# Turning normed rows among the last product steps of each projection in a one-core decoder step

## The chip, the core and the metric

The kernel runs on one core of a Trainium2 chip, in one launch. Its time is device microseconds of that core, the median of several executions. A core has TensorE (PE) for matrix products and transposes, VectorE (DVE), ScalarE (ACT), GpSimd (POOL) and SyncE (SP), which issues most transfers. Each works through its own instructions in order, and they wait for one another by semaphores.

## What is computed

One inference step of a two-layer decoder trunk: 512 prompt rows and 8 x 8 sample rows of width 1024. Layer 0 mixes by block-sparse and sliding-window attention, layer 1 by gated linear attention (GLA). Each layer has a convolutional feed-forward part of inner width 2816. Four times the residual stream goes through a layer norm, after the attention's output projection, after the first down projection, after the GLA output projection and after the second down projection:

```python
xp = layer_norm(DN_ALPHA * xp + mp, ln_mix_g[l], ln_mix_b[l])
fp, cbp = conv_ffn(xp, buf0, ffn_w_up[l], ffn_conv_w[l], ffn_conv_b[l], ffn_w_down[l])
xp = layer_norm(DN_ALPHA * xp + fp, ln_ffn_g[l], ln_ffn_b[l])
```

The output of each of the first three norms is the input of the next projection (up projection of layer 0, GLA's q and k, up projection of layer 1). The fourth is the result.

## The kernel before

**Tiles.** The rows lie in five tiles, 0 to 3 of 128 prompt rows and 4 (PQ) of the 64 sample rows. Products are done in fp32r in three parts: a matrix is split into a high part (rounded, `xh_reg`, `w_hi`) and a low part (what is left, `xl_reg`, `w_lo`), and a step multiplies high by high, high by low and low by high. A weight unit is 512 KB, loaded by SP (L475, L587) into `raw`. ACT makes `w_hi` (L1138, L1283), DVE makes `w_lo` (L1475, L1745), and for the first unit behind a norm POOL makes it (`split_after_norm`, L2052).

**Product steps with a norm behind them** (`products_before_norm`). A step (c, t) multiplies weight unit c with tile t into PSUM bank t, with L669 for prompt tiles and L680 for the sample rows. The last two units are walked as pairs, in the order of `PAIR`; here 0 and 1 stand for the last unit but one and the last:

```python
PAIR = [(0, 0), (0, 1), (1, 0), (0, 2), (1, 1), (0, 3), (1, 2), (0, 4), (1, 3), (1, 4)]
```

For a norm behind two units (stage 0) each is a half of the width, and DVE reads a bank after every step. For stages 1 and 2 both belong to the second half, and DVE reads a bank only after (1, t). A full step of a prompt tile is 12 products of 512 columns, the last of stages 1 and 3 has 6. A step of the sample rows has 8 or 4.

**The norm on DVE** (`residual_ln`). `residual` adds the bank to the residual rows (L1666, for the sample rows also L1670) and takes statistics (L1673). `normalise` joins them (L1679), subtracts the mean and multiplies by the gain (L1684), waits for ACT's square root (L1255, `ln_roots`), and does the rest (L1686, L1688), which signals `ln_done`.

**Turning** (`turn_x`, `turn`, L650). The normed rows have to stand with the width on the partitions. PE transposes a tile in two batches of four 128 x 128 blocks, into PSUM banks 5 and 6 in turn. A batch waits until ACT has copied the one before last out (L1124, `take_x`, the high part), and, where that was a normed tile, until DVE has taken the low part (L1482, `x_los`).

**The hand-over** (`run_here`, `after_ln`, `lo_here`). The first unit behind the norm has four runs, m = 0 to 3, of 24 products of 288 columns. Runs 0 and 1 read columns 0 to 287 (tiles 0, 1 and a part of 2), runs 2 and 3 the rest. Ahead of m = 0 PE waits for this unit's `w_lo`, then turns tiles 0, 1 and 2 and waits for their low parts. Ahead of m = 1 it turns tile 3, ahead of m = 2 tile 4, and it waits there for all parts. DVE has the low parts of tiles 0 to 2 behind the norm of tile 3, and those of 3 and 4 behind the norm of tile 4. ACT copies tiles 0 to 2 behind the root of tile 3, and 3 and 4 behind the root of tile 4. It makes `w_hi` of the next unit behind the root of tile 2, once step (0, 4) has been done.

**Side rows** (`turn_sides`, `take_sides`). The up projections also need 20 rows of convolution state, weights and biases feature-major: two batches of 22 transposes of 20 x 128 blocks. In stages 0 and 2 PE does them just ahead of the step that is fifth from the end, (0, 3), and ACT copies them behind the root of tile 1.

Batches of transposes are numbered in the order in which PE does them (`BATCH_LN0`, `BATCH_LN1`, `BATCH_Y`, `BATCH_LN2`, `LO_BATCHES`), and waits are counted by these numbers.

Of the kernel before, what the change touches and what calls it, by code (L numbers as in the profile page):

```python
# [21 lines left out]
NTILE = len(TILES)  # L22
# [38 lines left out]
KEY_STEPS = [(tile_, g_) for tile_ in range(2) for g_ in range(4)]  # L61
# [24 lines left out]
for k_, n_ in (("attn_out", 2), ("down0", 2 * len(DOWN_GROUPS)), ("gla_out", 4), ("down1", 2 * len(DOWN_GROUPS))):  # L86
    NORM_UNITS.append([UNIT_NO[(k_, c_)] for c_ in range(n_)])
PAIRED = {units_[-2] for units_ in NORM_UNITS}


def freed(n):
# [71 lines left out]
def build_program(nc, io):  # L163
    with ExitStack() as ctx:
# [242 lines left out]
        def query_tile(n):  # L407
# [10 lines left out]
        KEYS_TURNED = {step: BATCH_BEFORE_SAMPLE + sum(2 * GROUP_BLOCKS[g] for _, g in KEY_STEPS[:i + 1])  # L418
                       for i, step in enumerate(KEY_STEPS)}

        BATCH_LN0 = KEYS_TURNED[KEY_STEPS[-1]] + 2 * SP_BATCH + 2
        BATCH_LN1 = BATCH_LN0 + TURNS_X
        BATCH_GLA = BATCH_LN1 + TURNS_X
        BATCH_Y = BATCH_GLA + 2 * GH
        BATCH_LN2 = BATCH_Y + TURNS_X + 2

        LO_BATCHES = ([b for b in range(TURNS_X)]
                      + [b0 + b for b0 in (BATCH_LN0, BATCH_LN1, BATCH_Y, BATCH_LN2) for b in range(TURNS_X)])

        def state_place(n):  # L430

# [206 lines left out]
        def _(pe):  # L638
# [245 lines left out]
            def products_before_norm(stage, groups, before_tile=None):  # L884


                sums = norm_sums(stage)
                for c, t in norm_steps(stage):
                    n = NORM_UNITS[stage][c]
                    half, g = divmod(c, len(groups(0)))  # L890
                    k0, kn = groups(c)[g]
                    unit_here(n)
                    if stage % 2 == 0 and (c, t) == norm_steps(stage)[-5]:
                        turn_sides(stage // 2)
                    if before_tile is not None:
                        before_tile(c, t)
                    if half == 1 and g == 0:
                        pe.wait_ge(z_read, 2 * stage * NTILE + sums.index((0, t)) + 1)
                    project(n, t, k0, kn, g == 0, g == len(groups(0)) - 1)

            def samples_here(c, t):
                if t == PQ:
# [10 lines left out]
            def run_here(m, stage, first_batch):  # L913


                if m == 0:
                    after_ln(stage, range(3))
                    lo_here(first_batch, 6)
                elif m == 1:
                    after_ln(stage, [3])  # L920
                elif m == 2:
                    after_ln(stage, [4])
                    pe.wait_ge(turned_out, first_batch + TURNS_X)
                    lo_here(first_batch, TURNS_X)

            def ffn(l):
# [191 lines left out]
        def _(act):  # L1118
# [132 lines left out]
            def ln_roots(stage):  # L1251
                for t in range(NTILE):
                    n = TILES[t][1]
                    act.wait_ge(ln_var, stage * NTILE + t + 1)
                    act.activation(ln_sd[0:n, t, 0:1], ln_mv[0:n, t, 1:2], ACT.Sqrt, bias=eps_ln[0:n, 0:1]).then_inc(ln_root, 1)  # L1255
                    if stage % 2 == 0 and t == 1:
                        take_sides()
                    if t == 2 and stage < 3:
                        split_hi(NORM_UNITS[stage][-1] + 1)
                    if t == 3 and stage < 3:  # L1260
                        for before in range(3):
                            take_x(before)
                if stage < 3:
                    take_x(3)
                    take_x(4)

            def take_sides():
                for v in range(2):
# [193 lines left out]
        def _(dve):  # L1462
# [23 lines left out]
            def x_los(first_batch, t):  # L1486

                r0, n = TILES[t]
                for half in range(2):
                    k0 = 4 * half  # L1490
                    in_order, beside_hi = xTl[:, k0:k0 + 4, r0:r0 + n], xTh[:, k0:k0 + 4, NT:SLOT]
                    if t < PQ or first_batch in (BATCH_LN0, BATCH_LN2):
                        places = [in_order]
                    elif first_batch == BATCH_LN1:
                        places = [beside_hi, in_order]
                    else:
                        places = [beside_hi]
                    batch_lo(first_batch + 2 * t + half, k0, r0, n, places)

            split_lo(0)  # L1500
            for t in range(NTILE):
# [188 lines left out]
            def residual_ln(stage, duty, first_batch):  # L1690
# [5 lines left out]
                for i, (c, t) in enumerate(norm_steps(stage)):  # L1696
                    if t == 0 and c < len(units) - 1:
                        duty(c)
                    half, late = divmod(c, per_half)
                    if late < per_half - 1:  # L1700
                        continue
                    sums += 1
                    residual(stage, half, t, STEPS_BEFORE[units[0]] + i + 1, 2 * stage * NTILE + sums)
                    if half == 1:
                        normalise(stage, t)
                        if t == 3 and first_batch is not None:

                            for before in range(3):
                                x_los(first_batch, before)
                if first_batch is not None:  # L1710
                    x_los(first_batch, 3)
                    x_los(first_batch, 4)
                    dve.wait_ge(lo_done, units[-1] + 2)

            def units_of(kind, n):
# [474 lines left out]
```

## Time and profile before

| | us |
|---|---|
| median of three executions | 1608.63 (1607.99 to 1610.58) |
| the profiled execution | 1606.65 |
| its span in the profile | 1604.9 |
| PE busy with products and transposes | 1508.3 (94%) |
| DVE busy | 920.0 (57%) |
| ACT busy | 553.4 (34%) |
| POOL busy | 57.1 (4%) |
| share of PE in the chain that ended last | 85% |
| mean granted clock of TensorE | 0.971 |

A timeline row gives start (us from the start of the span), duration, engine, line, operation, output and inputs, sizes, count, and in brackets how long the engine had been idle and what released it. The granted clock is the share of 2.4 GHz, so 0.50 is 1.2 GHz. Matmul ends are modelled, and the next product starts before the last has ended, so the distance of starts is what a product costs.

### The profile page before, as it was taken

Reading aid. Unit: us, or ns where it says so; the run is one execution under the profiler, and the core shown is the slowest. Engines: PE = TensorE matmul, PEld = TensorE weight load, DVE = VectorE, ACT = ScalarE, POOL = GpSimd, SP = SyncE. Lnnn points to the kernel's source line nnn. Section 1 sums busy time; section 2 is a strip of 40 time slices with the busy share of each in tenths; the row PEclk is TensorE's granted clock in tenths of the full one; section 3 lists DMA queues with packets and bytes.
Section 4 is the critical chain, followed back from the end, with each engine's and each line's share of the span. In section 5 each row is a group of like instructions: output and inputs, shape, how many; then the busy total and the mean of one; then the engine's idle time right before and its main releaser. Section 6 shows DMA issues by size and latency. Waiting matters only on the chain.

```text
span 1604.9 us, 24203 instructions
## 1 busy us (share of the span) xinstructions
PE 1508.3 (94%) x9372; PEld 1331.2 (83%) x9372; DVE 920.0 (57%) x1738; ACT 553.4 (34%) x1030; POOL 57.1 (4%) x90
## 2 busy tenths in 40 slices
PE   6999897889999999999799999899899999999995
PEld 5888675669999999878698888668799999998784
DVE  2654253377666666554721776575676666665545
ACT  3222276324333333332225332521243333333321
POOL 0002200010000000000100000000100000000000
PEclk9999999989999999999899999999799999999998
DMA  5225456622223321422211211442022333214211
GB/s 174 102 99 163 115 203 232 171 73 80 79 82 90 88 80 52 129 79 92 78 55 53 79 53 53 136 150 80 27 80 79 84 90 87 79 52 128 79 66 59
DMA packets 153215, 153.56 MB, mean 96 GB/s; under 512 B 12014, under 2 KB 122734, under 8 KB 152910
## 3 DMA queue, kind: packets, MB, share of 16 engines
q1 hardware_dynamic: 149210, 139.47, 28.1%
q0 software_dynamic: 3936, 13.14, 2.6%
q8 instruction: 47, 0.77, 0.2%
q14 instruction: 22, 0.18, 0.0%
HBM read 140.76 MB, written 21.91 MB: 101 GB/s over the span
## 4 chain that ended last, share of the span: by engine, by line
PE 85%; DVE 7%; ACT 3%; SPq 2%; issue 2%; DMA 1%; POOL 0%; ACTq 0%; DVEq 0%; POOLq 0%
PE ps L669 69%; PE ps L680 4%; PE ps L650 4%; PE ps L1026 1%; DVE x_reg L1684 1%; PE ps L737 1%; PE ps L1059 1%; PE ps L771 1%; SPq L522 1%; PE ps L1090 1%; DVE x_reg L1688 1%; DVE w_lo L1475 1%; ACT w_hi L1138 1%; PE ps L947 1%; DVE x_reg L1666 1%
## 5 line engine op out<-in xcount | busy, mean ns | idle before, releaser
L669 PE MATMUL ps<-xh_reg,w_hi 128*128 128x288 f32 x1552 | 465.4, 300 | 8.2 <-DVE xl_reg L1482 8.2
L669 PE MATMUL ps<-xl_reg,w_hi 128*128 128x288 f32 x1552 | 460.8, 297 | 0.0
L669 PE MATMUL ps<-xh_reg,w_lo 128*128 128x288 f32 x1552 | 460.8, 297 | 0.0
L669 PE MATMUL ps<-w_hi,xh_reg 128*128 128x512 f32 x768 | 308.2, 401 | 6.9 <-DVE xl_reg L1726 3.4
L669 PEld LDWEIGHTS ps<-xh_reg,w_hi 128*128 128x128 f32 x1552 | 295.1, 190 | 10.5 <-DVE xl_reg L1482 5.4
L669 PE MATMUL ps<-w_hi,xl_reg 128*128 128x512 f32 x768 | 302.2, 394 | 0.0
L669 PE MATMUL ps<-w_lo,xh_reg 128*128 128x512 f32 x768 | 302.1, 393 | 0.0
L669 PEld LDWEIGHTS ps<-xl_reg,w_hi 128*128 128x128 f32 x1552 | 295.3, 190 | 0.0
L669 PEld LDWEIGHTS ps<-xh_reg,w_lo 128*128 128x128 f32 x1552 | 294.9, 190 | 0.0
L1475 DVE TENSOR_TENSOR w_lo<-raw,w_hi 128x2048 fp32r<-128x2048 f32 (+1 forms) x52 | 113.7, 2186 | 259.1 <-ACT w_hi L1138 259.1
L669 PEld LDWEIGHTS ps<-w_hi,xh_reg 128*128 128x128 f32 x768 | 146.3, 191 | 39.0 <-issue 7.2
L1138 ACT ACTIVATE w_hi<-raw 128x2048 fp32r<-128x2048 f32 (+1 forms) x55 | 100.8, 1833 | 223.2 <-PE ps L680 215.0
L669 PEld LDWEIGHTS ps<-w_hi,xl_reg 128*128 128x128 f32 x768 | 145.9, 190 | 31.4
L1761 DVE TENSOR_SCALAR arena<-arena 128x512 f32<-128x512 f32 (+1 forms) x176 | 67.7, 427 | 179.3 <-ACT arena L1297 179.3
L1763 DVE SCALAR_TENSOR_TENSOR arena<-arena 128x512 f32<-128x512 f32 x352 | 166.8, 515 | 6.3
L669 PEld LDWEIGHTS ps<-w_lo,xh_reg 128*128 128x128 f32 x768 | 146.3, 191 | 28.9
L1296 ACT ACTIVATE arena<-ps 128x224 f32<-128x224 f32 x88 | 31.5, 358 | 239.4 <-PE ps L669 239.4
L1745 DVE TENSOR_TENSOR w_lo<-raw,w_hi 128x2048 fp32r<-128x2048 f32 x44 | 100.5, 2284 | 3.3 <-ACT w_hi L1283 3.1
L1283 ACT ACTIVATE w_hi<-raw 128x2048 fp32r<-128x2048 f32 x44 | 83.7, 1902 | 0.1
L680 PE MATMUL ps<-w_hi,xh_reg 128*128 128x512 f32 x192 | 75.8, 395 | 1.3 <-DVE x_reg L1670 1.3
L650 PE MATMUL ps<-ident,x_reg 128*128 128x128 f32 (+1 forms) x232 | 40.9, 335 | 38.1 <-DVE xl_reg L1482 12.2
L1294 ACT ACTIVATE arena<-ps 128x288 f32<-128x288 f32 x88 | 36.0, 412 | 112.7 <-PE ps L669 112.7
(188 smaller groups left out, 1530.5 us busy)
## 6 DMA issues: line engine op xcount, KB each, us to landing
raw<-in_ffn_w_up SPq DMA_DIRECT2D x88, 512.0 KB, 5.0
raw<-in_ffn_w_down SPq DMA_DIRECT2D x40, 512.0 KB, 4.6
raw<-in_attn_w_in SPq DMA_DIRECT2D x24, 512.0 KB, 4.8
raw<-in_gla_w_in SPq DMA_DIRECT2D x24, 512.0 KB, 4.6
out_swa_s<-in_state_swa_kv SPq DMA_DIRECT2D x2, 3968.0 KB
x_reg<-in_x_prompt SPq DMA_DIRECT2D x8, 512.0 KB, 7.1
raw<-in_gla_w_out SPq DMA_DIRECT2D x8, 512.0 KB, 4.7
out_swa_p<-arena POOLq DMA_DIRECT2D x18, 128.0 KB, 3.0
```

The costliest lines, as they stand in the source:

```text
L522: sp.dma_start(values_of[s][:, b:b + GROUP_BLOCKS[g], :] if g < 3 else values_of[s][:, b, :], src).then_inc(v_cached[s // 4], 16)
L650: last = pe.transpose(ps[0:cols, bank, col:col + rows], src, ident[0:rows, 0:rows])
L669: mm = pe.matmul(out, lhs(i, a), rhs(i, b), start=first and i == 0 and a + b == 0, stop=last and i == ks - 1 and a == 1)
L680: mm = pe.matmul(ps[:, t, :], xTh[:, k0 + i, NP:SLOT], w[b][:, i, :], start=first and i + b == 0, stop=last and i == kn - 1 and b == 1)
L1138: act.activation(w_hi[:, n % 2, 0:a], raw[:, n % 2, 0:a], ACT.Copy).then_inc(hi_done, 1)
L1283: act.activation(w_hi[:, slot, :], raw[:, slot, :], ACT.Copy).then_inc(hi_done, 1)
L1294: act.activation(ext[:, u, v, 2:2 + SPLIT], ps[:, m, 0:SPLIT], ACT.Copy).then_inc(ext_ready, 1)
L1296: act.activation(ext[:, u, v, 2 + SPLIT:2 + NP], ps[:, m, 0:PRE], ACT.Copy)
L1475: dve.tensor_tensor(w_lo[:, n % 2, 0:a], raw[:, n % 2, 0:a], w_hi[:, n % 2, 0:a].bitcast(F32), ALU.subtract).then_inc(lo_done, 1)
L1745: dve.tensor_tensor(w_lo[:, slot, :], raw[:, slot, :], w_hi[:, slot, :].bitcast(F32), ALU.subtract).then_inc(lo_done, 1)
L1761: ins = dve.tensor_scalar(y, e, w, fj[:, u, v, SIDE - 1:SIDE], ALU.mult, ALU.add)
L1763: ins = dve.scalar_tensor_tensor(y, e, w, y, ALU.mult, ALU.add)
```

## The change

In stages 0 to 2 PE turns tile 0 behind step (1, 1), tile 1 behind (1, 2) and tile 2 behind (1, 3), each after a wait for the norm of that tile. At m = 0 it then only waits for the low parts of tiles 0 to 2. The side rows are turned at m = 2, ahead of tile 4. ACT copies tiles 0 and 1 behind their own roots, tile 2 behind `w_hi`, and tile 3 and the side rows behind the root of tile 3, all ahead of the root of tile 4. DVE takes the low parts of tiles 0 and 1 behind the norms of tiles 1 and 2, those of tile 2 ahead of the norm of tile 3, and those of tile 3 ahead of the norm of tile 4. The numbers of the batches follow. Stage 3, which has no projection behind it, stays.

```diff
+TURN_STEPS = (-6, -4, -2)
...
-        BATCH_LN0 = KEYS_TURNED[KEY_STEPS[-1]] + 2 * SP_BATCH + 2
-        BATCH_LN1 = BATCH_LN0 + TURNS_X
+        BATCH_LN0 = KEYS_TURNED[KEY_STEPS[-1]] + 2 * SP_BATCH
+        BATCH_LN1 = BATCH_LN0 + TURNS_X + 2
...
-        BATCH_LN2 = BATCH_Y + TURNS_X + 2
+        BATCH_LN2 = BATCH_Y + TURNS_X
...
-                      + [b0 + b for b0 in (BATCH_LN0, BATCH_LN1, BATCH_Y, BATCH_LN2) for b in range(TURNS_X)])
+                      + [b0 + b + (2 if b0 in (BATCH_LN0, BATCH_LN2) and b >= 8 else 0)
+                         for b0 in (BATCH_LN0, BATCH_LN1, BATCH_Y, BATCH_LN2) for b in range(TURNS_X)])
...
-                    if stage % 2 == 0 and (c, t) == norm_steps(stage)[-5]:
-                        turn_sides(stage // 2)
                     if before_tile is not None:
                         before_tile(c, t)
                     if half == 1 and g == 0:
                         pe.wait_ge(z_read, 2 * stage * NTILE + sums.index((0, t)) + 1)
                     project(n, t, k0, kn, g == 0, g == len(groups(0)) - 1)
+                    for before, at in enumerate(TURN_STEPS):
+                        if stage < 3 and (c, t) == norm_steps(stage)[at]:
+                            pe.wait_ge(ln_done, stage * NTILE + before + 1)
+                            turn_x(before)
...
                 if m == 0:
-                    after_ln(stage, range(3))
                     lo_here(first_batch, 6)
                 elif m == 1:
                     after_ln(stage, [3])
                 elif m == 2:
+                    if stage % 2 == 0:
+                        turn_sides(stage // 2)
                     after_ln(stage, [4])
-                    pe.wait_ge(turned_out, first_batch + TURNS_X)
+                    pe.wait_ge(turned_out, first_batch + TURNS_X + (0 if stage % 2 else 2))
                     lo_here(first_batch, TURNS_X)
...
-                    if stage % 2 == 0 and t == 1:
-                        take_sides()
-                    if t == 2 and stage < 3:
+                    if stage == 3:
+                        continue
+                    if t < 2:
+                        take_x(t)
+                    elif t == 2:
                         split_hi(NORM_UNITS[stage][-1] + 1)
-                    if t == 3 and stage < 3:
-                        for before in range(3):
-                            take_x(before)
-                if stage < 3:
-                    take_x(3)
-                    take_x(4)
+                        take_x(2)
+                    elif t == 3:
+                        take_x(3)
+                        if stage % 2 == 0:
+                            take_sides()
+                    else:
+                        take_x(4)
...
                     if half == 1:
+                        if t >= 3 and first_batch is not None:
+                            x_los(first_batch, t - 1)
                         normalise(stage, t)
-                        if t == 3 and first_batch is not None:
-
-                            for before in range(3):
-                                x_los(first_batch, before)
+                        if 1 <= t < 3 and first_batch is not None:
+                            x_los(first_batch, t - 1)
                 if first_batch is not None:
-                    x_los(first_batch, 3)
-                    x_los(first_batch, 4)
+                    x_los(first_batch, NTILE - 1)
                     dve.wait_ge(lo_done, units[-1] + 2)
```

## Rows read from the trace of the kernel before

**Rows 1.** Waits of PE: who waited for whom, total us, times, longest.
```profile
PE ps L650 <- DVE xl_reg L1482: 14.1, 7, 5.8
```

**Rows 2.** Timeline of PE at the hand-over of stage 0.
```profile
323.41 2.88 PE L650 MATMUL ps<-ident,arena 20*128 20x20 f32 x44 [0.78 <-issue]
326.22 0.80 PE L669 MATMUL ps<-w_hi,xh_reg 128*128 128x512 f32 x1
...
330.63 0.39 PE L669 MATMUL ps<-w_hi,xh_reg 128*128 128x512 f32 x1
...
339.38 0.47 PE L680 MATMUL ps<-w_hi,xh_reg 128*128 128x512 f32 x1 [1.34 <-DVE x_reg L1670]
...
342.48 1.09 PE L650 MATMUL ps<-ident,x_reg 128*128 128x128 f32 x8 [1.02 <-POOL w_lo L2052]
...
351.13 0.61 PE L669 MATMUL ps<-xh_reg,w_hi 128*128 128x288 f32 x1 [1.41 <-DVE xl_reg L1482]
...
357.01 1.03 PE L650 MATMUL ps<-ident,x_reg 128*128 128x128 f32 x8
357.80 0.38 PE L669 MATMUL ps<-xh_reg,w_hi 128*128 128x288 f32 x1
...
361.13 0.71 PE L650 MATMUL ps<-ident,x_reg 64*128 64x64 f32 x8
362.94 0.37 PE L669 MATMUL ps<-xh_reg,w_hi 128*128 128x288 f32 x1 [1.10 <-DVE xl_reg L1482]
```

**Rows 3.** Windows: stretch, us, busy of PE, PEld, DVE, ACT, POOL, PEclk, DMA share, GB/s.
```profile
40.00:62.00 22.00, 22.00 (x108) 17.91 (x107) 15.37 (x24) 4.59 (x6) 0.54 (x1) 1.00 0.40 138
...
326.30:329.30 3.00, 3.00 (x7) 2.40 (x8) 0.91 (x1) 0.54 (x1) 0.00 (x0) 0.50 0.58 166
...
351.10:356.90 5.80, 5.77 (x24) 5.77 (x25) 4.77 (x7) 0.29 (x1) 0.00 (x0) 0.50 0.00 0
...
811.10:814.10 3.00, 3.00 (x13) 3.00 (x13) 2.29 (x1) 0.46 (x1) 0.00 (x0) 0.50 0.00 0
```

**Rows 4.** Timeline of DVE, POOL and PE at the hand-over of stage 1.
```profile
775.49 1.28 DVE L1688 SCALAR_TENSOR_TENSOR x_reg<-x_reg,ln_sd,arena 128x1024 f32<-128x1024 f32 x1
...
784.92 4.79 POOL L2052 TENSOR_TENSOR w_lo<-raw,w_hi 128x2048 fp32r<-128x2048 f32 x1 [126.99 <-ACT w_hi L1138]
...
786.95 3.84 DVE L1684 SCALAR_TENSOR_TENSOR x_reg<-x_reg,ln_mv,arena 128x1024 f32<-128x1024 f32 x1
...
798.88 0.61 PE L669 MATMUL ps<-xh_reg,w_hi 128*128 128x288 f32 x1 [1.41 <-DVE xl_reg L1482]
...
808.61 0.71 PE L650 MATMUL ps<-ident,x_reg 64*128 64x64 f32 x8
811.08 0.58 PE L669 MATMUL ps<-xh_reg,w_hi 128*128 128x288 f32 x1 [1.76 <-DVE xl_reg L1482]
```

**Rows 5.** Timeline of PE at the hand-over of stage 2.
```profile
1127.90 0.50 PE L669 MATMUL ps<-w_hi,xh_reg 128*128 128x512 f32 x1
...
1153.23 0.61 PE L669 MATMUL ps<-xh_reg,w_hi 128*128 128x288 f32 x1 [1.41 <-DVE xl_reg L1482]
...
1165.06 0.37 PE L669 MATMUL ps<-xh_reg,w_hi 128*128 128x288 f32 x1 [1.10 <-DVE xl_reg L1482]
```

**Rows 6.** Timeline of DVE, ACT and POOL at the hand-over of stage 0.
```profile
322.85 0.67 DVE L1666 SCALAR_TENSOR_TENSOR x_reg<-x_reg,ps 128x512 f32<-128x512 f32 x1
...
324.52 0.30 ACT L1255 ACTIVATE ln_sd<-ln_mv,eps_ln 128x1 f32<-128x1 f32 x1 [5.30 <-DVE ln_mv L1679]
...
325.92 1.28 DVE L1688 SCALAR_TENSOR_TENSOR x_reg<-x_reg,ln_sd,arena 128x1024 f32<-128x1024 f32 x1
326.33 0.54 ACT L1124 ACTIVATE arena<-ps 128x440 f32<-128x440 f32 x1 [0.83 <-PE ps L650]
...
337.88 4.54 POOL L2052 TENSOR_TENSOR w_lo<-raw,w_hi 128x2048 fp32r<-128x2048 f32 x1 [139.80 <-ACT w_hi L1138]
...
344.82 1.28 DVE L1482 TENSOR_TENSOR xl_reg<-ps,xh_reg 128x512 fp32r<-128x512 f32 x2
```

More of the change, by code:

```diff
@@ L1497, in x_los @@
                         places = [beside_hi]
-                    batch_lo(first_batch + 2 * t + half, k0, r0, n, places)
+                    batch_lo(LO_BATCHES[LO_BATCHES.index(first_batch) + 2 * t + half], k0, r0, n, places)
             split_lo(0)
```

## The prediction

> **What bounds the kernel now.** TensorE carries the chain that ends last (85% of it, the page's section 4). The waits view shows where it still loses time at the norms: the transposes L650 wait 14.1 us in 7 waits for DVE's low parts L1482 [rows 1]. I then read the timeline of the three hand-overs from a norm to the next projection. I call norm t Nt, the eight transposes of a normed tile Tt, the four runs of the first unit behind them m0 to m3, and the two side batches S.
>
> Hand-over 0: S sits between (1,1) and (0,3), 2.88 us, and the twelve products of (0,3) behind it take 330.63 - 326.22 = 4.41 us, since they run at 1.2 GHz for 3 us [rows 2, 3]; twelve at full clock take 2.72 (12 x 0.227). (1,4) starts at 339.38 because DVE read the sample rows' first half late. T0 starts at 342.48, released by POOL's w_lo and not by N0, which is long done. T0, T1, T2 then alternate with ACT's and DVE's splits, and m0 starts at 351.13, its 24 products at 1.2 GHz taking 5.8 us; m2 starts at 362.94 [rows 2]. Hand-over 1 has no S: POOL ends at 789.71, m0 starts at 798.88, m2 at 811.08 [rows 4]. Hand-over 2 is like 0: m0 at 1153.23, m2 at 1165.06 [rows 5]. From m2 on PE runs without a gap, so what m2 gains reaches the end, if the next weights keep up.
>
> **Prices.** T between products: T3 starts at 357.01, the next product at 357.80, T3 itself is 1.03 long [rows 2]; bounds 0.79 and 1.03, I take 0.85. Residual with norm on DVE: 322.85 to 327.20, 4.3 us; the residual alone is two operations of 0.67 to 0.69 with their issue, 1.45, so the norm is 2.85. Low parts of a tile: 1.28, with issue 1.3. POOL's w_lo: 4.54 to 4.8 [rows 4, 6]. Nothing is computed more or less: per norm the ten turns of four transposes, the 44 transposes of S and the ten splits stay. Added are three waits on PE for N0, N1 and N2, and behind each stand the remaining product steps.
>
> **Hand-over 0, changed.** T0 behind (1,1) finds N0 done; (0,3) starts near 323.3 instead of 326.22 and stays at full clock, so (1,2) starts near 326.0 instead of 330.63. N1 ends at 327.20 as before [rows 6], so T1, behind (1,2), has no wait. Now DVE is the pace: from 327.1, low parts of tile 0 (1.3) to 328.4, first half of tile 3 (1.45) to 329.85, tile 2 and N2 (4.3) to 334.1, low parts of tile 1 to 335.4. T2's second bank needs those, so PE waits about 1.1 us there. The sample half's sum is read at 336.8, and (1,4) starts at 336.95 instead of 339.38. DVE: 337.55, tile 3's sum 339.0, low parts of tile 2 340.3. ACT's w_hi may start after (0,4), 331.7; POOL's w_lo ends at 338.2, covered. So m0 starts near 340.35, 10.8 us earlier. N3 (2.85) follows the low parts and ends at 343.1; at full clock m0 takes 3.2 us (24 x 0.132), so N3 is just hidden. T3, m1: to 347.7.
>
> Here the change gives back. On ACT the root of the sample rows stands behind the taking of S, and PE turns S only at m2. S ends at 350.75 (2.9 us), its second copy (0.54, starting 0.1 behind S [rows 6]) at 351.4, root 0.3, DVE's last norm operation 1.28 and about 0.25 for the reciprocal ahead of it: 353.2. T4 to m2 took 362.94 - 361.13 = 1.81. So m2 starts at 355.05, where it was 362.94: **7.9 us**. Were the root ahead of S, it would be 2.5 more.
>
> **Hand-over 2, changed.** (0,3) started at 1127.90 behind S and at low clock; (1,2) now starts near 1128.55, 3.8 earlier. (1,2) 2.7, T1 0.85, (0,4) 1.8: 1134.1 by rounding up, where ACT's w_hi starts, some 1.9 long; POOL from 1136.05 to 1140.9. DVE: tile 2 from 1131.5, N2 1135.8, low parts of tile 1 1137.1, tile 3's sum and low parts of tile 2 1139.9. (1,4) ends 1139.5. POOL is last: m0 at 1140.95, 12.3 earlier. m1 ends 1148.2, S 1151.25, copy, root and norm 1153.7, T4 and its splits 1155.55, against 1165.06: **9.5 us**.
>
> **Hand-over 1, changed.** Steps are shorter (six products in the last group) and DVE never rests. N0 ends at 776.77 [rows 4], a few tenths behind (1,1), so T0 makes PE wait (0.5 by my schedule); T1 waits as long for tile 0's low parts. (0,4) then ends some 2.4 us later than before (two T at 0.85 and these waits), w_hi with it, and POOL's w_lo, from 784.92 to 786.85, ends at 791.65. DVE has three pairs of low parts ahead of N3: 4.0 us, so its last one is done at 790.7. m0 starts at 791.7, 7.2 earlier, still at low clock, 5.6 us as now (a little under the 5.8 of hand-over 0). N3's first operation, 3.84 us long now because it stands while POOL works [rows 4], is done at 792.75, N3 at 794.2. T3 at 797.3; N4 now follows tile 3's low parts: T3's copies and low parts take some 2.5 from its start, to 799.85, and N4 2.95, to 802.8, while m1 (0.85 for T3, 3.2 for itself) is over by 801.5, so m2's wait has a new last member. T4 to m2 took 811.08 - 808.61 = 2.47: 805.3, **5.8 us** earlier.
>
> **Clock.** Together 23.2 us. The waits at m2 with S last 7.3 us, hold no product, and will bring the clock down to 1.2 GHz, which in the profile of before it was not at m2 of hand-overs 0 and 2 [rows 2]. Products behind such waits ran at 0.50 for 3.0 (m2 of hand-over 1, start 811.08) to 5.8 us (m0) [rows 3]: half of that is lost, 1.5 to 2.9; the wait is long, I take 2.5 twice, 5.0. At m0 of hand-over 0 PE now has only (1,4) and T2 in 6.2 us: nothing to 2.6 lost, I take 1.5. At m2 of hand-over 1 the wait grows from 2.5 to 3.8 us: nothing to 1.4 more, I take 0.7. Net 23.2 - 7.2 = 16.0 us. The profiled execution took 1606.65 (span 1604.9), 2.0 below the median of 1608.63: 1590.65 for it, **1592.6** for the median.
>
> Queues passed: on ACT, w_hi waits behind T1's copies, 0.1 us or nothing. SP's next weight load hangs on POOL's w_lo: 4.2 us earlier in hand-over 0, 1.9 later in hand-over 1, where it has the 12 us of m0 to m3. The w_lo of the unit behind m3 follows T4 on ACT and DVE as before, and keeps its cover of m2 and m3, 6.4 us; uncovered it would show as a wait ahead of the second unit.
>
> **A rule against it.** Turns of four transposes stand between the product steps of the first projection, and the clock is 1.00 over those 22 us [rows 3]. S, 2.8 us of transposes without a gap, was followed by 0.50. The Trainium skill ("TensorE: Matmul & The Clock Gate", Part 4, PE-mode transpose) says that transposes don't count as busy PE in the way products do; the second row agrees. By that rule the waits at m2 stay idle for the clock even while S runs, which is what I charged by the rows; if T0 to T2 tipped it too, the third rival below would be the time.
>
> **Rivals.**
> 1. The clock falls wherever it can: also at both m0 (2.6 each), 2.9 behind both S, 1.4 in hand-over 1. Gain 23.2 - 12.4 = 10.8: 1597.8. For: PE is mostly idle there. Against: T0 at 342.48, behind 1.34 and 1.02 us of idle, still took 1.09, as at full clock [rows 2]. 0.20.
> 2. The clock is kinder: m0 of hand-over 1 at full clock (2.4 more) and 1.6 lost behind each S. Gain 22.4: 1586.2. 0.10.
> 3. Slower: the transposes between products pull the clock down from T0 to the end of m1. Products at full clock there are 18.2 us in hand-overs 0 and 2 and 11.3 in 1; at half clock 47.7 us more, less the 23.2, plus the 5 behind S: 29.5 slower, 1638. It decides from 38% of that stretch (18.2 of 47.7). Against: the 22 us with turns at 1.00 [rows 3]. 0.03.
> 4. No gain: the earlier start only moves the wait, to weights of the second unit or to the sample rows' norm, by some 5 us more in each hand-over than I see. 1606 to 1609. Against: the cover above. 0.04.
>
> **Numbers.** The forecast has 0.63: 1589 to 1596. 0.2% of this time, 3.2 us, is what a measurement can tell from no change. Forecast and rivals 1 and 2 are faster: 0.93; rival 4 is 0.04 within, rival 3 is 0.03 slower. The range of 8 in 10 reaches from rival 2's 1586 beyond rival 1 to 1602, for a few waits of 1 us that a schedule by hand misses.
>
> **What would show it.** Right: T0, T1, T2 between products; m0 starts 11, 7 and 12 us earlier relative to (1,1) of the same norm; ACT's last root behind the copies of S; the longest wait of a transpose at T4 in hand-overs 0 and 2; m2 there at 0.50. Wrong: clock below 1.00 between T0 and (1,4); m0 released by something other than DVE's low parts (0) or POOL (1, 2); a wait ahead of the second unit.

## The result, and the profile after

The changed kernel takes **1592.22 us**, the median of 4 runs (1586.38 to 1593.65), against 1609.35 for 4 runs of the kernel before (1607.99 to 1610.58): a ratio of 0.989, 95% interval 0.9876 to 0.9904. That is 17.1 us less; forecast were 16.0 and 1592.6. The profiled execution of the changed kernel took 1593.65 (span 1591.9), the slowest of its four; the one of before was faster than all four of its kernel, so the two traces differ by only 1604.9 - 1591.9 = 13.0 us.

First the waits of PE, columns as in [rows 1]. The lines have moved: L650 is L654, L669 is L673, L680 is L684, L1482 is L1492, L1666 is L1676, L1688 is L1698, L2052 is L2061.

```profile
PE ps L654 <- DVE xl_reg L1492: 11.0, 5, 6.7
...
PE ps L654 <- DVE x_reg L1698: 6.2, 4, 2.3
...
PE ps L673 <- POOL w_lo L2061: 3.5, 2, 2.2
```

The transposes' wait for low parts was 14.1 us in 7 waits [rows 1] and is 11.0 in 5; 9.6 of it lies outside the three hand-overs, and within them 0.34 and 1.05 us are left, both at T2. New are the waits of T4 for the norm of the sample rows (2.31 us in hand-overs 0 and 2, 1.22 in 1) and those of m0 for POOL. Next the timeline of PE at hand-over 0, against [rows 2]:

```profile
324.82 1.04 PE L654 MATMUL ps<-ident,x_reg 128*128 128x128 f32 x8
...
337.10 1.22 PE L654 MATMUL ps<-ident,x_reg 128*128 128x128 f32 x8 [0.34 <-DVE xl_reg L1492]
...
339.01 0.47 PE L684 MATMUL ps<-w_hi,xh_reg 128*128 128x512 f32 x1 [0.69 <-DVE x_reg L1680]
...
342.36 0.37 PE L673 MATMUL ps<-xh_reg,w_hi 128*128 128x288 f32 x1 [1.27 <-DVE xl_reg L1492]
...
349.73 2.95 PE L654 MATMUL ps<-ident,arena 20*128 20x20 f32 x44
354.98 1.11 PE L654 MATMUL ps<-ident,x_reg 64*128 64x64 f32 x8 [2.31 <-DVE x_reg L1698]
357.12 0.58 PE L673 MATMUL ps<-xh_reg,w_hi 128*128 128x288 f32 x1 [1.02 <-DVE xl_reg L1492]
```

From the top: T0 stands between products; T2 waits 0.34 us; (1,4) starts at 339.01, released by DVE's sum; m0 at 342.36, released by DVE's low parts; then S (349.73), T4 and m2. The first row of m0 takes 0.37 us where it took 0.61, the first of m2 0.58: m0 has the full clock, m2 has not. In hand-overs 1 and 2 (timeline of PE) POOL releases m0, as foreseen:

```profile
788.38 0.37 PE L673 MATMUL ps<-xh_reg,w_hi 128*128 128x288 f32 x1 [2.25 <-POOL w_lo L2061]
...
793.16 1.03 PE L654 MATMUL ps<-ident,x_reg 128*128 128x128 f32 x8
...
801.05 0.58 PE L673 MATMUL ps<-xh_reg,w_hi 128*128 128x288 f32 x1 [1.76 <-DVE xl_reg L1492]
...
1135.29 0.40 PE L673 MATMUL ps<-xh_reg,w_hi 128*128 128x288 f32 x1 [1.27 <-POOL w_lo L2061]
...
1150.04 0.58 PE L673 MATMUL ps<-xh_reg,w_hi 128*128 128x288 f32 x1 [1.02 <-DVE xl_reg L1492]
```

Busy time by window (columns as in [rows 3], PEclk the granted clock) says where it was full:

```profile
324.00:336.00 12.00, 12.00 (x63) 10.10 (x62) 11.65 (x18) 4.63 (x7) 0.00 (x0) 1.00 0.52 141
336.00:342.00 6.00, 4.06 (x20) 2.56 (x18) 5.87 (x10) 1.24 (x3) 4.67 (x2) 1.00 0.00 1
342.00:348.00 6.00, 5.64 (x44) 5.67 (x45) 5.83 (x10) 1.38 (x3) 0.00 (x0) 1.00 0.66 178
...
352.70:362.70 10.00, 6.69 (x31) 6.54 (x32) 4.58 (x5) 4.32 (x10) 0.00 (x0) 0.50 0.04 9
```

To see where 13.0 us came from I cut each trace at six points: the read of (1,0)'s second half by DVE, and the first product of m2, in each hand-over. The first interval of a hand-over is its "length" below; its unit is us.

| kernel | to (1,0) | hand-over 0 | between | hand-over 1 | between | hand-over 2 | to the end | span |
|---|---|---|---|---|---|---|---|---|
| before | 317.23 | 45.71 | 409.46 | 38.68 | 308.64 | 45.34 | 439.84 | 1604.9 |
| after | 319.58 | 37.54 | 411.97 | 31.96 | 312.98 | 36.01 | 441.86 | 1591.9 |
| difference | +2.35 | -8.17 | +2.51 | -6.72 | +4.34 | -9.33 | +2.02 | -13.0 |

The hand-overs give 24.2 us. Behind them 2.5, 0.95 (of the 4.34) and 2.0 go to m2 and m3, whose first 5.6, 5.4 and 4.5 us ran at half clock (before: 0, 3.2 and 0). The other 3.4 behind hand-over 1 and the 2.35 ahead of hand-over 0 lie where nothing was changed. The largest piece, 2 us, shows in windows at the same place of both programs, four small gate projections (this kernel, then before):

```profile
856.00:861.00 5.00, 4.99 (x14) 3.37 (x13) 0.00 (x0) 2.67 (x6) 0.00 (x0) 0.66 0.31 118
```

```profile
865.00:870.00 5.00, 4.00 (x17) 2.38 (x15) 0.00 (x0) 3.67 (x9) 0.00 (x0) 0.89 0.35 136
```

The clock is 0.66 there, where it was 0.89. By the granted clock it was low from 857.6 to 867.9 us, and in the kernel before from 868.9 to 875.8. Ahead of hand-over 0 it is the same: low from 280.8 to 291.0 us, and before from 281.8 to 288.7.

### The profile page after: what moved, and what is told of

It is laid out like the page before. It is cut to its first block, busy times and chain, and to the rows that moved or that the text cites. A ratio compares the mean times of both kernels' runs of the same rounds, so it can differ in the third digit from the quotient of the medians.

```text
span 1591.9 us, 24205 instructions
## 1 busy us (share of the span) xinstructions
PE 1501.7 (94%) x9372; PEld 1326.6 (83%) x9372; DVE 915.1 (57%) x1738; ACT 552.9 (35%) x1030; POOL 56.7 (4%) x90
## 4 chain that ended last, share of the span: by engine, by line
PE 85%; DVE 6%; ACT 3%; issue 2%; SPq 2%; DMA 1%; POOL 1%; ACTq 0%; DVEq 0%; POOLq 0%
PE ps L673 68%; PE ps L684 5%; PE ps L654 4%; PE ps L1033 1%; PE ps L741 1%; PE ps L1066 1%; PE ps L775 1%; ACT w_hi L1145 1%; SPq L526 1%; PE ps L1097 1%; DVE x_reg L1694 1%; DVE w_lo L1485 1%; DVE x_reg L1698 1%; DVE xl_reg L1492 1%; PE ps L954 1%
## 5 line engine op out<-in xcount | busy, mean ns | idle before, releaser
L673 PE MATMUL ps<-xh_reg,w_hi 128*128 128x288 f32 x1552 | 465.6, 300 | 8.6 <-DVE xl_reg L1492 5.1
L673 PE MATMUL ps<-xl_reg,w_hi 128*128 128x288 f32 x1552 | 461.2, 297 | 0.0
L673 PE MATMUL ps<-xh_reg,w_lo 128*128 128x288 f32 x1552 | 461.2, 297 | 0.0
L673 PE MATMUL ps<-w_hi,xh_reg 128*128 128x512 f32 x768 | 307.8, 401 | 6.9 <-DVE xl_reg L1735 3.4
L673 PEld LDWEIGHTS ps<-xh_reg,w_hi 128*128 128x128 f32 x1552 | 295.3, 190 | 11.0 <-issue 6.2
L673 PE MATMUL ps<-w_hi,xl_reg 128*128 128x512 f32 x768 | 301.9, 393 | 0.0
L673 PE MATMUL ps<-w_lo,xh_reg 128*128 128x512 f32 x768 | 301.9, 393 | 0.0
L673 PEld LDWEIGHTS ps<-xl_reg,w_hi 128*128 128x128 f32 x1552 | 295.4, 190 | 0.0
L673 PEld LDWEIGHTS ps<-xh_reg,w_lo 128*128 128x128 f32 x1552 | 295.0, 190 | 0.0
L673 PEld LDWEIGHTS ps<-w_hi,xh_reg 128*128 128x128 f32 x768 | 146.0, 190 | 39.1 <-issue 7.2
L673 PEld LDWEIGHTS ps<-w_hi,xl_reg 128*128 128x128 f32 x768 | 145.6, 190 | 31.1
L673 PEld LDWEIGHTS ps<-w_lo,xh_reg 128*128 128x128 f32 x768 | 146.0, 190 | 28.6
L684 PE MATMUL ps<-w_hi,xh_reg 128*128 128x512 f32 x192 | 76.4, 398 | 0.7 <-DVE x_reg L1680 0.7
L684 PE MATMUL ps<-w_lo,xh_reg 128*128 128x512 f32 x192 | 75.0, 391 | 0.0
```

The source lines that it names most:

```text
L673: mm = pe.matmul(out, lhs(i, a), rhs(i, b), start=first and i == 0 and a + b == 0, stop=last and i == ks - 1 and a == 1)
L684: mm = pe.matmul(ps[:, t, :], xTh[:, k0 + i, NP:SLOT], w[b][:, i, :], start=first and i + b == 0, stop=last and i == kn - 1 and b == 1)
```

## The experiments

Theory: PE's order at each hand-over made T0 to T2 wait for POOL and then for one another; turned between products they wait for little (0.39 us at T0 in hand-over 1, 0.34 and 1.05 at T2). What is left are a root that stands late on ACT (2.3 us twice) and the clock at m2 (2 to 2.5 us twice, 1 once). Rivals: S's move did it; all of it came with T0 alone; or what was lost behind m2 is something other than the clock. Each kernel has its median, its ratio to the kernel before as it was measured beside it (medians 1608.94 for runs 1 to 4, 1608.54 for 5 to 8, 1608.96 for 9 to 12), and the lengths of hand-overs 0, 1 and 2 from its trace. No run turns T0 alone, so the second rival is tested for T2 only (run 12).

**1. The changed kernel again, without an edit.**

> The changed kernel once more, nothing edited. I measure a hand-over from DVE's first read behind step (1,0) (L1676, the residual of tile 0) to the first product of m2: 37.54, 31.96 and 36.01 us in the profiled execution of the changed kernel, 45.71, 38.68 and 45.34 before. If the schedule of semaphores sets these, they come back within 0.5 us. If the 3.4 us that were lost between the hand-overs 1 and 2 of the profiled execution (clock at 0.50 one microsecond earlier at the four small projections of the gate, and at the first steps of the GLA output) come from when the clock happens to fall, that loss is different here, 0 to 5 us; if the change causes it, it is again 3 to 4 us.

1593.32 us, 0.9899 (0.9883 to 0.9916); 37.50, 31.96, 36.01. The hand-overs repeat to 0.04 us, and the loss behind hand-over 1 to 0.1 (313.09 us between). By the expectation that speaks for the change as the cause of this loss; runs 3 and 11 speak against it (below). The four executions here and the four of the result lie up to 8 us apart; two of the eight have a trace, so where these differ isn't shown.

**2. The root of the sample rows ahead of the side copies on ACT.**

```diff
                         take_x(3)
-                        if stage % 2 == 0:
-                            take_sides()
                     else:
+                        if stage % 2 == 0:
+                            take_sides()
                         take_x(4)
```

> ACT takes the root of the sample rows ahead of the copies of the side rows, in hand-overs 0 and 2. My theory: the root is the last member of the wait at m2, so both hand-overs shorten by 2.3 us, the idle time ahead of T4 (37.54 to 35.2, 36.01 to 33.7), hand-over 1 stays at 31.96; the clock still falls ahead of m2. 4.6 us less than the changed kernel, some 1587.6. Rival, that the wait ahead of T4 is for DVE's norm itself and not for the root: no change, 1592. Rival, that a shorter wait also spares the fall of the clock: 5 us more, 1583.

1585.62 us, 0.9853 (0.9836 to 0.9869); 35.38, 31.96, 33.66: shorter by 2.16, 0 and 2.35, as expected. Time fell by 6.6 us (7.7 against run 1), 2 to 3 more than forecast. The clock still fell, but less of the low stretch lies behind the start of m2: 4.5, 3.4 and 3.4 us, for 5.6, 5.4 and 4.5. That makes the products from m2 on 0.5, 0.9 and 0.5 us faster; the rest lies elsewhere. In hand-over 2 (PE timeline) m2 starts at full clock, and runs at half clock from its third product to 1147.0:

```profile
1143.33 0.37 PE L673 MATMUL ps<-xh_reg,w_hi 128*128 128x288 f32 x1 [1.02 <-DVE xl_reg L1492]
...
1143.71 0.44 PE L673 MATMUL ps<-xh_reg,w_lo 128*128 128x288 f32 x1
...
1147.06 0.29 PE L673 MATMUL ps<-xl_reg,w_hi 128*128 128x288 f32 x1
```

**3. The kernel before with S at m = 2, and nothing else of the change.**

```diff
-                    if stage % 2 == 0 and (c, t) == norm_steps(stage)[-5]:
-                        turn_sides(stage // 2)
...
                 elif m == 2:
+                    if stage % 2 == 0:
+                        turn_sides(stage // 2)
                     after_ln(stage, [4])
```

ACT's side copies move from the root of tile 1 to the copies of tile 3, behind all roots, and the numbers of the batches follow.

> The kernel before, with only the side rows moved to m2 (turns of tiles 0 to 2 stay ahead of m0, all roots stay ahead of the copies). My theory: (0,3) starts 3 us earlier and at full clock, but the turns of tiles 0 to 2 still follow POOL's w_lo one after the other, and at m2 PE now pays 2.9 us for the side rows and loses 1.5 to 2.5 to the clock. Hand-overs 0 and 2 are 43 to 45 us (45.7 and 45.3 before), the time within 3 us of the kernel before, 1606 to 1611. Rival, that the side rows' place is where the gain comes from (their 2.9 us and the low clock behind them among the steps): 8 us or more faster, under 1601.

1608.23 us, 0.9989 (0.9973 to 1.0005), no difference; 43.13, 39.05, 43.28. S's move takes 4.65 and 4.68 us from the way to m0 (29.25 and 28.83 us behind (1,0), where it was 33.90 and 33.51) and gives half of it back at m2. Between hand-overs 1 and 2 this trace has 311.66 us, 3.0 more than before, though T0 to T3 stand where they stood.

**4. The changed kernel with S back ahead of T0.**

```diff
+                    if stage % 2 == 0 and (c, t) == norm_steps(stage)[-6]:
+                        turn_sides(stage // 2)
                     for before, at in enumerate(TURN_STEPS):
...
-                    if stage % 2 == 0:
-                        turn_sides(stage // 2)
                     after_ln(stage, [4])
```

ACT copies the side rows behind the root of tile 1 here, ahead of tiles 0 and 1.

> The changed kernel with the side rows back among the steps, behind (1,1) and ahead of T0. My theory: (0,3) is late again by 2.9 us and runs at low clock, and since DVE's reads follow it, m0 comes 4 to 5 us later; at m2 the side rows and the late root are gone, 5.2 us of wait less, and the clock falls for less or not at all. Hand-overs 0 and 2 within 1.5 us of 37.5 and 36.0, the time 1588 to 1593: the new place of the side rows is worth little by itself. Rival, that the new place carries the gain: 1600 or more.

1592.34 us, 0.9886 (0.9858 to 0.9914), equal to the change; 40.03, 31.96, 35.00. Hand-over 0 is outside what I expected (by 1.0 us), and m0 comes 6.5 us later there and 3.3 in hand-over 2, where I had 4 to 5 for both. In hand-over 0 S first waits 0.93 us for a transfer, then runs 3.23 us at a falling clock, which stays low from 327.6 to 334.4. In hand-over 2 S stands in the same place and the clock is 1.00 throughout (1116 to 1152). The window's clock, and S in the timeline of PE:

```profile
325.22 3.23 PE L654 MATMUL ps<-ident,arena 20*128 20x20 f32 x44 [0.93 <-DMA arena<-in_ffn_conv_b]
```

```profile
324.00:335.00 11.00, 10.07 (x67) 8.70 (x66) 6.11 (x9) 2.56 (x5) 0.00 (x0) 0.69 0.50 137
```

Runs 3 and 4 together: the rival with S falls. The gain comes with T0 to T2 and the order of copies and low parts that they allow; no run parts these.

**5. The sample rows' norm ahead of tile 3's low parts.**

```diff
-                        if t >= 3 and first_batch is not None:
+                        if t == 3 and first_batch is not None:
                             x_los(first_batch, t - 1)
                         normalise(stage, t)
...
-                    x_los(first_batch, NTILE - 1)
+                    x_los(first_batch, 3)
+                    x_los(first_batch, 4)
```

with ACT's copies of tile 3 and of the side rows behind the last root.

> The changed kernel with the norm of the sample rows ahead of the low parts of tile 3 on DVE, and its root ahead of the copies of tile 3 and of the side rows on ACT: the order of the kernel before for these. In hand-over 1 DVE stood idle 1.64 us ahead of tile 3's low parts, waiting for T3; N4 fits in there, and ends some 1.5 us earlier. My theory: hand-over 1 shortens from 31.96 by 1.1 us, the wait ahead of T4; hand-overs 0 and 2 shorten as with the root first alone, 1.6 to 2.3 us each, since S now waits up to 0.7 us for tile 3's low parts. In all 4.5 to 5.7 us less, some 1587. Rival, that the order chosen by the change is better there: 1592 or more.

1587.25 us, 0.9864 (0.9848 to 0.9881); 37.69, 30.68, 34.50. Hand-over 1 as expected, 2 nearly so, 0 not (35.2 to 35.9 expected). The trace shows why (timeline of PE): S needs the bank that tile 3's low parts empty, so it now waits 1.09 us for them, and that wait sits where the clock falls: S takes 4.05 us instead of 2.95.

```profile
350.10 4.05 PE L654 MATMUL ps<-ident,arena 20*128 20x20 f32 x44 [1.09 <-DVE xl_reg L1491]
```

**6. S ahead of T2.** The two lines of `turn_sides` move from m = 2 to the wait for N2.

ACT copies the side rows behind `w_hi`, ahead of tile 2.

> The changed kernel with the side rows turned behind (1,3), ahead of T2, where PE waits for DVE (0.34 ahead of T2, 0.7 ahead of (1,4), 1.3 ahead of m0 in hand-over 0). My theory: the side rows' 2.9 us are covered there in hand-over 0 but for about 1 us, in hand-over 2 but for 2.4 us; the wait at m2 loses the side rows and the late root. Hand-over 0: 37.54 - 3 = 34.5; hand-over 2: 36.01 - 1.2 = 34.8; the clock falls for less at m2, or at m0 instead. 4 to 7 us less, 1585 to 1588. Rival, that the pace at T2 is already critical so that the side rows are paid in full: 1590 or more.

1587.19 us, 0.987 (0.985 to 0.989); 36.57, 30.42, 34.74. Hand-over 2 as expected, 0 not (34.5): PE was idle there 0.34 us only, and 1.8 us into S the clock fell; it was low from 338.7 to 345.5, through the rest of S, T2 and (1,4), so that PE, not DVE, set m0 (26.2 us behind (1,0) for 22.8). Hand-over 1, in which nothing is edited, is 30.42 us for 31.96: its m0 kept the full clock (24 products in 3.2 us for 4.8). So that the time lies in the range is in part luck: 0.97 and 1.27 us come from the edit, 1.54 from a clock that it doesn't touch. Windows and timeline of PE:

```profile
336.00:347.00 11.00, 10.66 (x74) 9.48 (x73) 9.28 (x15) 2.57 (x5) 4.63 (x2) 0.69 0.36 98
```

```profile
336.93 3.58 PE L654 MATMUL ps<-ident,arena 20*128 20x20 f32 x44 [0.34 <-DVE xl_reg L1492]
340.44 1.97 PE L654 MATMUL ps<-ident,x_reg 128*128 128x128 f32 x8
```

**7. The waits at m = 2 filled with useless products.** They go into a bank that nobody reads.

```diff
+            def keep_busy(count):
+
+                for i in range(count):
+                    pe.matmul(ps[:, 7, 0:HALF], xTh[:, i % KD, 0:P], xTh[:, i % KD, 0:HALF], start=True, stop=True)
...
                         turn_sides(stage // 2)
+                        keep_busy(10)
                     after_ln(stage, [4])
+                    keep_busy(4)
```

> The changed kernel with 10 products of 512 columns, of no use, between the side rows and T4 in hand-overs 0 and 2, and 4 behind T4 in all three, into PSUM bank 7, which nobody reads then: 2.3 and 0.9 us at full clock, inside the waits of 2.31 and 1.0 (1.76 in hand-over 1). My theory: the clock at m2 is what costs 2.5, 0.95 and 2.0 us behind the three hand-overs; kept up it gives back 4 to 5 us: 1587 to 1588, hand-overs within 0.3 us of now, and PEclk 1.00 at m2. Rival, that products in so short a stretch don't hold the clock: hand-overs longer by up to 1 us each, since the products themselves then run at half clock, 1592 to 1595.

1583.29 us, 0.9845 (0.9828 to 0.9861), 9 us below the change and better than forecast; 37.30, 30.42, 35.79. The lengths hardly change (1.5 in hand-over 1, whose m0 stays at full clock, as it did in run 6 without a filler); between and behind them are 409.41, 310.13 and 439.82 us, 2.6, 2.9 and 2.0 less than after. Most of the gain is m2 and m3 at full clock: 2.5, 2.4 and 2.0 us. I had counted only 0.95 for hand-over 1, what it lost against before, where half of that m2 was at low clock too. With the clock at 1.00 the first 140 products from m2 on take 18.66 us in hand-overs 0 and 2, as in the kernel before, where they took 21.15 and 20.69 after the change: the loss behind m2 there is the clock and nothing else. PE at hand-over 0, timeline and window:

```profile
351.42 2.56 PE L922 MATMUL ps<-xh_reg 128*128 128x512 f32 x10
353.91 0.71 PE L654 MATMUL ps<-ident,x_reg 64*128 64x64 f32 x8
354.56 1.20 PE L922 MATMUL ps<-xh_reg 128*128 128x512 f32 x4
355.73 0.37 PE L673 MATMUL ps<-xh_reg,w_hi 128*128 128x288 f32 x1
```

```profile
354.00:364.00 10.00, 10.00 (x74) 9.46 (x75) 6.76 (x12) 5.55 (x13) 0.00 (x0) 1.00 0.33 93
```

**8. POOL makes only half of `w_lo`.** This one leaves out the low part of half the unit's columns (what was there before stays).

> The changed kernel, but POOL makes only the first half of the columns of w_lo of the first unit behind each norm (the other half keeps what was there, so results behind it are off). POOL's operation falls from 4.6 to about 2.3 us. My theory: POOL releases m0 in hand-overs 1 and 2 (waits of 2.25 and 1.27), and holds N3's first operation 1.0 us longer. m0 then follows the low parts of tile 2: 1.3 us earlier in both, but T3 and N4 hang on N3, 1.0 earlier: hand-over 1 is 30.7 to 31.0, hand-over 2 34.7 to 35.0, hand-over 0 stays. 2 to 3 us less, 1589 to 1590. Rival, that POOL is not on the path: 1592.

1588.55 us, 0.9877 (0.9861 to 0.9894); 37.51, 29.37, 34.75. Hand-over 0, where DVE releases m0, doesn't move; the other two are 2.59 and 1.26 shorter, m0 1.29 and 1.22 earlier, and DVE releases both. POOL is the bound of m0 there by just that much, and the other 1.3 in hand-over 1 is the clock of its m0, which stays full; as it does so in run 6 with POOL's whole `w_lo`, it can't be put down to this edit. POOL, and N3's first operation on DVE, in this trace:

```profile
783.92 2.39 POOL L2062 TENSOR_TENSOR w_lo<-raw,w_hi 128x1024 fp32r<-128x1024 f32 x1 [129.12 <-ACT w_hi L1145]
...
787.28 1.28 DVE L1694 SCALAR_TENSOR_TENSOR x_reg<-x_reg,ln_mv,arena 128x1024 f32<-128x1024 f32 x1
```

**9. Runs 2 and 7 together**, with `keep_busy(2)` behind S.

> Both remedies together: the root of the sample rows ahead of the side copies on ACT, and useless products in PE's wait (now 2 behind S in hand-overs 0 and 2, 4 behind T4 in all three; the ten behind S would be in the way now). If the late root and the clock are two separate losses, the gains add: hand-overs 35.1, 30.4 and 33.5 us, the clock at 1.00 through m2 in all three, and 1578 to 1580 us (warm alone 1583.3, less 2.2 and 2.3). If it was the ten products behind S that held the clock in hand-over 0, m2 there runs at 0.50 again and the time is 1580.5 to 1582.

1581.44 us (1580.99 to 1584.49), 0.9828 (0.9812 to 0.9845), 36.99, 30.44, 34.30: the fastest median, though its interval overlaps that of runs 7 and 11. But the sum didn't come; the time is the rival's. In hand-over 0 the clock is low from 352.5 to 359.3, and the useless products, now at half clock (2.07 us for four, which took 1.20), stand in m2's way: the hand-over is 1.6 us longer than in run 2. But the rival's cause, that two products don't hold what ten held, isn't shown there: S ends at 352.4 and the clock falls at 352.5, while the two are running and before a third would have started. In hand-over 2 it falls at 1140.9, when eight more would have been running; there the rival may hold.

```profile
353.46 1.11 PE L654 MATMUL ps<-ident,x_reg 64*128 64x64 f32 x8
354.50 2.07 PE L922 MATMUL ps<-xh_reg 128*128 128x512 f32 x4
```

**10. The same, and in hand-over 1 the sample rows' norm ahead of tile 3's low parts.**

> The same, and in hand-over 1 alone the sample rows' norm ahead of tile 3's low parts (there it won 1.28 us before, and there is no S in the way). Hand-over 1 at 29.1 to 29.3 us, the others as in the run without it, and 1.2 to 1.3 us less: 1577 to 1579 us. If PE is still busy with m1 when the norm is done, less than 0.5 us comes of it.

1584.84 us, 0.9849 (0.9833 to 0.9865); 36.92, 29.96, 34.45. A miss: hand-over 1 gains 0.48 us for the 1.2 expected, since T4's first batch now waits for the low parts of tile 3 that hold its bank (timeline of PE). In run 5 the same order won 1.28 us because m0 ran at low clock, 1.5 us longer, and T4 came when those low parts were done.

```profile
794.81 0.43 PE L654 MATMUL ps<-ident,x_reg 64*128 64x64 f32 x4 [0.79 <-DVE xl_reg L1502]
```

The median is 3.4 us above run 9's, though their profiled executions are 0.5 apart. That I can't explain.

**11. Useless transposes for the useless products of run 7**, 20 and 9 of 128 columns.

```diff
-                    pe.matmul(ps[:, 7, 0:HALF], xTh[:, i % KD, 0:P], xTh[:, i % KD, 0:HALF], start=True, stop=True)
+                    pe.transpose(ps[:, 7, i % 4 * P:i % 4 * P + P], ident[:, :], ident[:, :])
```

> The useless products of the warm run replaced by useless transposes of about the same length (20 and 9 of 128 columns, ident against ident, into the same bank). If transposes do not hold the clock as products do, m2 runs at 0.50 as without them and the time is 1591 to 1594 us. If any work on PE holds it, m2 runs at full clock and the time is 1583 to 1585 us.

1582.82 us (1580.73 to 1583.82), 0.9835 (0.9819 to 0.9852): as with products; 38.76, 30.42, 35.68. In hand-over 0 the clock was low from 351.0 to 354.4, through most of the twenty (4.02 us; 2.40 in hand-over 2, where it didn't fall), and was back before m2, though PE had done nothing but transposes since m1 (PE timeline, and windows):

```profile
351.06 4.02 PE L922 MATMUL ps<-ident 128*128 128x128 f32 x20
...
356.82 0.37 PE L673 MATMUL ps<-xh_reg,w_hi 128*128 128x288 f32 x1
...
1137.13 2.40 PE L922 MATMUL ps<-ident 128*128 128x128 f32 x20
```

```profile
351.00:353.00 2.00, 2.00 (x11) 1.97 (x11) 1.06 (x2) 0.72 (x2) 0.00 (x0) 0.50 0.00 0
...
355.00:357.00 2.00, 2.00 (x19) 1.75 (x19) 0.76 (x2) 1.47 (x3) 0.00 (x0) 1.00 0.00 0
```

Full-width transposes bring back (hand-over 0) or hold (hand-over 2) the full clock for m2 here. That speaks against the rule of the Trainium skill ("TensorE: Matmul & The Clock Gate", Part 4, PE-mode transpose) that I leaned on for S.

**12. T2 back behind (1,4); T0 and T1 stay.** `TURN_STEPS = (-6, -4, -1)`.

> One of the three turns undone: T2 stands behind (1,4) again, T0 and T1 stay between the products. My theory (a turn behind the last product step puts its splits on the path where DVE is the pace, and costs nothing where POOL is) gives hand-over 0 at 38.8 to 39.1 us instead of 37.5 (low parts of tile 2 wait for T2, m0 1.3 later), hand-over 1 at 31.8 to 32.1 as before, since POOL's w_lo releases m0, and hand-over 2 at 36.6 to 37.3 instead of 36.0; 1594 to 1596.5 us. The rival, that all of the gain comes with T0 and T1 and T2's place is free, gives 37.5, 32.0, 36.0 and 1592 to 1593.5.

1592.12 us, 0.9895 (0.9878 to 0.9911), equal to the change; 40.35, 31.80, 36.26. The trace is with the theory in direction (hand-over 1 unmoved, 0 longer, by 2.81 where 1.3 to 1.6 were expected; 2 by 0.25, less than expected): without T2 there PE is idle for 2.23 us ahead of (1,4), and (1,4) runs at half clock. The time is the rival's. In the profiled execution the hand-overs are 2.9 us longer together, and more than that came back elsewhere, 1.4 ahead of hand-over 0, 1.0 and 0.5 between the hand-overs and 0.4 behind the last, so the time can't tell the two apart: that T2's place is worth anything in the time isn't shown.

```profile
337.62 0.51 PE L684 MATMUL ps<-w_hi,xh_reg 128*128 128x512 f32 x1 [2.23 <-DVE x_reg L1680]
...
340.91 1.24 PE L654 MATMUL ps<-ident,x_reg 128*128 128x128 f32 x8
```

## Why the prediction was right, and where it wasn't

**The schedule held.** Taken relative to (1,0) of the same norm, m0 was forecast at 340.35, 791.7 and 1140.95 and came at 340.01, 791.69 and 1140.98: DVE as the pace of hand-over 0 and POOL as that of 1 and 2 were right, and run 8 shows the latter. At m2 the hand-overs gave 8.17, 6.72 and 9.33, for 7.9, 5.8 and 9.5: 24.2 for 23.2. T2's wait in hand-over 0 was 0.34 us, not 1.1: its first batch waits for the first half of tile 1's low parts (done at 336.95) and its second hardly for the other, where I had one wait, for both.

**The late root was there**, with its price: "2.5 more" for the root ahead of S was 2.16 and 2.35 in run 2.

**The clock was charged 1.8 us too much in sum, and wrong in places.** Charged were 1.5 at m0 of hand-over 0; nothing was lost (1.00 from T0 to the end of m0). m0 of hand-over 1 was forecast wholly at half clock, 5.6 us; it was low from 789.4 to 792.8 only, T3 came at 796.5 on the old scale instead of 797.3, and that is most of the 0.9 by which this hand-over beat its forecast. Behind m2, 2.5, 0.7 and 2.5 were charged; 2.5, 0.95 and 2.0 were lost. So 24.2 - 5.4 = 18.8 us net, where I had 16.0.

**Not foreseen** were 2.35 us ahead of hand-over 0 and 3.4 behind hand-over 1, in the profiled execution. The first is no part of the change: kernels that share all of the code up to there have 318.06 to 319.59 us, and run 3, which has the code of before there, 318.20. In all of them the clock was low for 10.2 us ahead of hand-over 0, in the trace of before for 6.8. The second comes again in run 1, but also in run 3 (311.66), which turns no tile among the products. In run 11, which has all three turns, the 2 us at the gate projections are gone (308.90 between, of which m2 at full clock is 1.45 less than before): the low stretch is 6.8 us there, as in before, and 10.2 in the other twelve traces. So neither the turns nor S's place sets it. I take it for the clock's own variation; before has one trace only, and no run isolates the rest.

That the forecast came within 1.1 us of the measured gain is partly luck. The schedule gave 1.0 us more than forecast and the clock took 1.8 less, so the steps make 18.8 net; unforeseen losses of 5.7 bring the pair of traces to 13.0, and the medians, 4.1 us better than this pair, to 17.1.

**Rivals.** The first (clock low wherever it can be) fell at the m0 of hand-overs 0 and 2, which stayed full. The second (kinder clock, 1586.2) has the time of one of the four executions (1586.38), which left no trace; in the trace m0 of hand-over 1 was low for only a part, and more than 1.6 us was lost behind each S. The third, that transposes between products pull the clock down, is excluded: 1.00 from 324 to 348, from T0 at 773.5 to 789.3, and from T0 at 1119.3 to 1147.7. The fourth (the gain only moves) fell: in hand-over 0 m2 starts 8.17 us earlier where m0 starts 11.12 earlier; the difference is S and the wait for the root (5.25 us together), less the 2.65 that a faster m0 gives back, and 0.3 at T4 and behind.

**The reason given for the clock at m2** stood on a weak leg: by the rule of the Trainium skill ("TensorE: Matmul & The Clock Gate", Part 4, PE-mode transpose) the wait counts as idle even while S runs. S, narrow transposes of 20 columns, was indeed followed by 0.50 (or ran into it) in most of these runs. Yet run 11 has full-width transposes in the same place doing what products do, and in hand-over 2 of run 4 S stands between products and the clock stays at 1.00. So it is not that transposes don't count at all. What of S does it, its 20-column width, the wait beside it or the moment at which it comes, no run here separates.

## What to carry to other kernels

Work that needs one engine's result and only prepares the next stage (here transposes of normed rows) belongs among the last steps of the stage that produces it, each at the first point where its input is ready by the trace; write the schedule of every engine by hand, and m0's start came out to 0.4 us here. On an in-order engine put the short step that releases others (a root of 0.28 us) ahead of the copies that nobody waits for: 2.2 us each time. Moving a wait is worth only what the next one allows (runs 3, 4, 5 and 10), and a wait in front of dense products can cost the clock on top: with the three waits at m = 2 filled with useless work the time was 9 us of 1592 lower (6.9 of them behind the start of the three m2), where the best reordering gave 6.6; where the clock falls all the same (run 9), the filler itself runs at half clock and stands in the way.

## What the runs showed of the hardware that was not expected

- Hand-overs repeat to 0.04 us between two executions of one kernel, while whole runs differ by up to 8 us. Yet hand-over 1, with the same instructions up to m2, is 31.96 us in runs 2 and 4 and 30.42 in run 6, since the clock falls in its m0 or doesn't. When the clock falls is the likely difference between executions too.
- Useless transposes of 128 columns served the clock as well as products of 512: 1582.82 against 1583.29 us.
- The same 44 transposes of S took 2.91 us at full clock (run 7), 3.23, 3.58 and 4.05 where the clock fell under them.
- POOL's subtraction goes by columns: 2.39 us for 128x1024, 4.55 for 128x2048. DVE's 128x1024 norm operation, which started while it ran, took 2.27 us in hand-over 1; in run 8, where POOL was done 0.98 us before it, 1.28:

```profile
783.73 4.55 POOL L2061 TENSOR_TENSOR w_lo<-raw,w_hi 128x2048 fp32r<-128x2048 f32 x1 [129.14 <-ACT w_hi L1145]
...
787.09 2.27 DVE L1694 SCALAR_TENSOR_TENSOR x_reg<-x_reg,ln_mv,arena 128x1024 f32<-128x1024 f32 x1
```
